# Experts' combination, final norm and the second mixer's norm in one stage over quarters of tokens

## The reference, cut to what matters

```python
# end of hier_moe: weighted sum of each token's two expert rows
y = yb[dest] * weights.reshape(-1)[order][:, None]
out = jax.ops.segment_sum(y, token_of, num_segments=t)
# end of the first block
x = x + g2x * hier_moe(...)
x = rmsnorm(x, final_norm_g)            # final norm of the first block
# start of the second block
h = x
z = rmsnorm_2(h, norm_mix_g[l]) @ w_in[l]     # the mixer's norm, then its input projection
...
h = h + jnp.concatenate([o_a, o_b, o_c], axis=-1) @ w_out[l]   # h is needed again here
```

## Time and profile before

| | |
|---|---|
| three runs | 4009.82, 4021.2, 4025.87 us; median 4021.2 |
| span of the profiled execution, first to last instruction | 4008.8 us |
| PE busy | 3340.9 us, 83% of the span |
| DVE busy | 2156.3 us, 54% |
| ACT busy | 1273.0 us, 32% |
| mean granted TensorE clock | 0.907 |
| bytes read and written | 449.40 MB and 79.38 MB |

### The profile page before, as it was taken

The page is one execution under the profiler, slowest core; times in us unless marked ns, Lnnn a source line. Parts: engine busy times, 40 slices in busy tenths (PEclk is TensorE's granted clock), DMA queues, the critical chain, the costliest instruction groups (busy, mean ns, idle before and its releaser), DMA issues. The chain is left out here.

```text
span 4008.8 us, 52023 instructions
## 1 busy us (share of the span) xinstructions
PE 3340.9 (83%) x18856; PEld 2686.1 (67%) x18856; DVE 2156.3 (54%) x3042; ACT 1273.0 (32%) x1914; POOL 210.2 (5%) x301
## 2 busy tenths in 40 slices
PE   5799884775969999996699868859488989998977
PEld 2688672664738888885488767638267877787755
DVE  3211643444359999997411175376436765776443
ACT  3201211335058888885300042421221110110011
POOL 1000000132001111110000000000000000000000
PEclk8899995788979999997899989969799999999988
DMA  6232641384149579995132212000203322332221
GB/s 241 72 93 65 180 150 57 96 224 142 44 172 374 204 261 382 373 359 186 43 104 89 74 66 61 27 29 4 79 16 94 94 80 86 96 93 80 68 63 42
DMA packets 381401, 507.45 MB, mean 127 GB/s; under 512 B 48218, under 2 KB 288465, under 8 KB 377953
## 3 DMA queue, kind: packets, MB, share of 16 engines
q1 hardware_dynamic: 342928, 439.80, 32.6%
q10 hardware_dynamic: 25856, 46.67, 3.3%
q0 software_dynamic: 12496, 19.35, 1.4%
HBM read 449.40 MB, written 79.38 MB: 132 GB/s over the span
## 5 line engine op out<-in xcount | busy, mean ns | idle before, releaser
L1923 DVE TENSOR_TENSOR exp_w_lo<-exp_w_raw,exp_w_hi 128x1024 fp32r<-128x1024 f32 x378 | 435.5, 1218 | 5.1
L1871 ACT ACTIVATE exp_w_hi<-exp_w_raw 128x1024 fp32r<-128x1024 f32 x378 | 371.0, 1055 | 7.7 <-PE exp_up_psum L339 7.7
L337 PE MATMUL in_ps_psum<-hN_hi,in_wh 128*128 128x512 f32 x704 | 276.4, 393 | 38.3 <-DVE in_wl L331 38.3
L337 PE MATMUL up_ps_psum<-hN_hi,up_wh 128*128 128x512 f32 x704 | 281.1, 399 | 31.0 <-DVE up_wl L331 31.0
L338 PE MATMUL up_ps_psum<-hN_lo,up_wh 128*128 128x512 f32 x704 | 280.7, 399 | 0.0
L339 PE MATMUL up_ps_psum<-hN_hi,up_wl 128*128 128x512 f32 x704 | 280.4, 398 | 0.0
L338 PE MATMUL in_ps_psum<-hN_lo,in_wh 128*128 128x512 f32 x704 | 275.8, 392 | 0.0
L339 PE MATMUL in_ps_psum<-hN_hi,in_wl 128*128 128x512 f32 x704 | 275.4, 391 | 0.0
L329 DVE CAST in_wh<-in_w 128x1024 fp32r<-128x1024 f32 x44 | 30.5, 694 | 424.2 <-PE in_ps_psum L339 414.2
L337 PE MATMUL exp_up_psum<-exp_w_hi,exp_x_hi 128*128 128x512 f32 x592 | 231.7, 391 | 3.6 <-DVE exp_w_lo L1923 3.6
L339 PE MATMUL exp_up_psum<-exp_w_hi,exp_x_lo 128*128 128x512 f32 x592 | 231.5, 391 | 0.0
(11 more groups left out here) (626 smaller groups left out, 7643.9 us busy)
## 6 DMA issues: line engine op xcount, KB each, us to landing
exp_w_raw<-in_expert_w_in SPq DMA_DIRECT2D x256, 512.0 KB, 5.7
up_w<-in_ffn_up SPq DMA_DIRECT2D x88, 512.0 KB
exp_w_raw<-in_expert_w_out SPq DMA_DIRECT2D x64, 512.0 KB, 7.0
hF<-in_expert_w_out SPq DMA_DIRECT2D x64, 512.0 KB, 7.3
ada_w<-in_ada_w SPq DMA_DIRECT2D x24, 1024.0 KB, 9.2
in_w<-in_w_in SPq DMA_DIRECT2D x44, 512.0 KB, 4.3
down_w<-in_ffn_down SPq DMA_DIRECT2D x44, 512.0 KB
wout_w<-in_w_out SPq DMA_DIRECT2D x16, 512.0 KB, 3.7
```

The costliest lines, as they stand in the source:

```text
L337: pe.matmul(out, r(w[0]), r(x[0]), start=start, stop=False)
L1871: act.activation(wh[:, c, :].bitcast(F32R), raw[c], ACT.Copy).then_inc(s_wh, 1)
L1923: dve.tensor_tensor(wl[:, c, :].bitcast(F32R), raw[c], wh[:, c, :], ALU.subtract).then_inc(s_wl[c], 1)
```

## The change

The three stages of combination, final norm and mixer's norm become one stage over four quarters of 256 tokens (two tiles each). The final norm is no longer written to `hF` there: the stage reads the un-normed `hF`, makes both means from one set of squares (a second matrix `gw` holds g1²/1024), writes the mixer's input (high and low) and keeps the first reciprocal root in `K.root1`. The normed `hF` is made later, by DVE, inside "in2" (`beside`, 16 instructions of 128x512). ACT's argument `aside` of `stage_gemm_f`, which nothing used, goes. The tiles of the routing plan stay allocated until the projection has ended.

```diff
@@ stage_gemm_f, list of DVE
                 weights(1, 0)
+                if beside is not None:
+                    beside(dve)
                 with dve.Fori(0, npair - 1) as i:
@@ stage_combine(K, x, gcol, g1, g2): list of ACT
+                def squares(q):
+                    act.wait_ge(s_h, 2 * q + 2)
+                    if q >= 2:
+                        act.wait_ge(s_st, q - 1)
+                    act.activation(sq[q % 2][:], cols(K.hF, q), ACT.Square).then_inc(s_sq, 1)
+
+                def first_root(q):
+                    u = q % 2
+                    act.wait_ge(s_st, q + 1)
+                    act.activation(ln1[u][:], p1[u][:, 0:QT], ACT.Ln, bias=K.c("eps")).then_inc(s_ln, 1)
+                    act.wait_ge(s_ln, q + 1)
+                    act.activation(inv1[u][:], ln1[u][:], ACT.Exp, scale=-1.0).then_inc(s_iv, 1)
+                    act.activation(K.root1[:, q * QT:(q + 1) * QT], ln1[u][:], ACT.Exp, scale=-0.5).then_inc(s_iv, 1)
+
+                def second_root(q):
+                    u = q % 2
+                    act.wait_ge(s_mx, q + 1)
+                    act.activation(ln2[u][:], ln2[u][:], ACT.Ln, bias=K.c("eps")).then_inc(s_l2, 1)
+                    act.wait_ge(s_l2, q + 1)
+                    act.activation(ln2[u][:], ln2[u][:], ACT.Exp, scale=-0.5).then_inc(s_rt, 1)
+
+                def high(q):
+                    act.wait_ge(s_x, 8 * q + 8)
+                    act.activation(cols(x[0], q).bitcast(F32R), tmp[q % 2][:], ACT.Copy).then_inc(s_hi, 1)
+                act.preload_act_table_set("natural_log_exp_and_others")
+                for i in range(3):
+                    weighted(i)
+                for q in range(NQ):
+                    squares(q)
+                    for i in (2 * q + 3, 2 * q + 4):
+                        if i < NT:
+                            weighted(i)
+                    first_root(q)
+                    second_root(q)
+                    if q:
+                        high(q - 1)
+                high(NQ - 1)
@@ list of DVE
+                def mixed(q):
+                    u = q % 2
+                    dve.wait_ge(s_iv, 2 * q + 2)
+                    dve.tensor_tensor(ln2[u][:], p2[u][:, 0:QT], inv1[u][:], ALU.mult).then_inc(s_mx, 1)
+
+                def normed(q):
+                    u = q % 2
+                    dve.wait_ge(s_rt, q + 1)
+                    dve.tensor_tensor(rr[u][:], ln2[u][:], K.root1[:, q * QT:(q + 1) * QT], ALU.mult).then_inc(s_mx2, 1)
+                    dve.wait_ge(s_mx2, q + 1)
...
+                    for k in range(KT):
+                        dve.scalar_tensor_tensor(tmp[u][:, k, :], cols(K.hF, q)[:, k, :], g12[:, k:k + 1], rr[u][:], ALU.mult, ALU.mult).then_inc(s_x, 1)
+
+                def low(q):
+                    dve.wait_ge(s_hi, q + 1)
+                    dve.tensor_tensor(cols(x[1], q).bitcast(F32R), tmp[q % 2][:], cols(x[0], q), ALU.subtract).then_inc(s_lo, 1)
+                dve.tensor_tensor(gsq[:], g1, g1, ALU.mult).then_inc(s_gn, 1)
+                dve.tensor_tensor(g12[:], g1, g2, ALU.mult).then_inc(s_gn, 1)
+                dve.wait_ge(s_gn, 2)
+                for k in range(KT):
+                    dve.tensor_scalar(gw[:, k, :], K.c("mean1024"), gsq[:, k:k + 1], None, ALU.mult).then_inc(s_gn, 1)
+                for i in range(2):
+                    summed(i)
+                for q in range(NQ):
+                    added(2 * q)
+                    if 2 * q + 2 < NT:
+                        summed(2 * q + 2)
+                    added(2 * q + 1)
+                    if 2 * q + 3 < NT:
+                        summed(2 * q + 3)
+                    if q:
+                        normed(q - 1)
+                    mixed(q)
+                    if q:
+                        low(q - 1)
+                normed(NQ - 1)
+                low(NQ - 1)
@@ list of PE
+                def means(q):
+                    u = q % 2
+                    pe.wait_ge(s_sq, q + 1)
...
+                    for k in range(KT):
+                        pe.matmul(p1[u][:, 0:QT], K.c("mean1024"), sq[u][:, k, :], start=k == 0, stop=k == KT - 1)
+                    for k in range(KT):
+                        mm = pe.matmul(p2[u][:, 0:QT], gw[:, k, :], sq[u][:, k, :], start=k == 0, stop=k == KT - 1)
+                    mm.then_inc(s_st, 1)
+                for i in range(3):
+                    turn(i)
+                for q in range(NQ):
+                    if 2 * q + 3 < NT:
+                        turn(2 * q + 3)
+                    means(q)
+                    if 2 * q + 4 < NT:
+                        turn(2 * q + 4)
@@ mixer_two(K, x)
-        x = tuple(K.sb(f"hN3_{x}", [P, KT, T], stack=norm) for x in ("hi", "lo"))
-        stage_norm(K, "nm", K.hF, x, T, K.cols[:, K.col_at["norm_mix_g_2"]:K.col_at["norm_mix_g_2"] + 8])
+        def residual_normed(dve):
+            for h in range(2):
+                t = slice(h * BANK, (h + 1) * BANK)
+                for k in range(KT):
+                    dve.scalar_tensor_tensor(K.hF[:, k, t], K.hF[:, k, t], K.col("final_norm_g", k), K.root1[:, t], ALU.mult, ALU.mult)
```

More of the change, by code:

```diff
@@ L451, in _, with stage_gemm_f @@
                     ada_vector(dve)
-def stage_gemm_f(K, name, groups, src, ntok, whole=None, residual=None, gcol=None, ctx=None, aside=None):
+def stage_gemm_f(K, name, groups, src, ntok, whole=None, residual=None, gcol=None, ctx=None, beside=None):
     npair = sum(g[1] for g in groups) // (2 * P)
@@ L533, in _ @@
                         mm.then_inc(s_mm[u], 1)
[L535 to L538, removed]
             if residual is None:
@@ L1948, in _, with stage_combine @@
                     rest_up(b, UP[3:])
-def stage_combine(K, gcol):
+def stage_combine(K, x, gcol, g1, g2):
     nc = K.nc
     yb = K.scratch["moe_y"]
-    NT, NB = T // P, 3
+    NT, NB, NQ = T // P, 3, 4
+    QT = T // NQ
     with K.stage() as st:
         U = range(2)
-        a = [[K.sb(f"comb_{k}_{u}", [P, D], stack=st) for u in range(NB)] for k in range(2)]
+        sb = lambda n, shape: K.sb(f"comb_{n}", shape, stack=st)
+        a = [[sb(f"{k}_{u}", [P, D]) for u in range(NB)] for k in range(2)]
+        sq, tmp = [sb(f"sq{u}", [P, KT, QT]) for u in U], [sb(f"tmp{u}", [P, KT, QT]) for u in U]
+        ln1, inv1, ln2, rr = ([sb(f"{n}{u}", [P, QT]) for u in U] for n in ("ln1", "inv1", "ln2", "root"))
+        gsq, g12, gw = sb("gain_sq", [P, KT]), sb("gains", [P, KT]), sb("gain_mean", [P, KT, P])
         pt = [K.ps(f"comb_ps{u}", [P, 2, 4, P], st) for u in U]
+        p1, p2 = ([K.ps(f"comb_{n}{u}", [P, BANK], st) for u in U] for n in ("mean", "gmean"))
         s_g = [[K.sem(f"comb_in{k}{u}") for u in range(NB)] for k in range(2)]
-        s_m, s_w, s_t, s_h = K.sem("comb_second"), K.sem("comb_sum"), K.sem("comb_turned"), K.sem("comb_added")
+        s_m, s_w, s_t, s_h, s_gn, s_sq, s_st, s_ln, s_iv, s_mx, s_l2, s_rt, s_x, s_hi, s_lo = (K.sem(f"comb_{n}") for n in (
+            "second", "sum", "turned", "added", "gains", "squares", "means", "log", "inverse", "mixed", "log2", "root", "normed", "hi", "lo"))
+        s_mx2 = K.sem("comb_roots")
+        cols = lambda t, q: t[:, :, q * QT:(q + 1) * QT]
         with nc.Block() as block:
@@ L1971, in _, with weighted @@
             def _(act):
-                for i in range(NT):
+                def weighted(i):
                     act.wait_ge(s_g[1][i % NB], 16 * (i // NB + 1))
                     act.activation(a[1][i % NB][:], a[1][i % NB][:], ACT.Copy, scale=K.moe_w[:, 1, i:i + 1]).then_inc(s_m, 1)
+                def squares(q):
[3 more added lines that the diff above has]
+                    act.activation(sq[q % 2][:], cols(K.hF, q), ACT.Square).then_inc(s_sq, 1)
@@ L1976, in _, with summed @@
+                high(NQ - 1)
             @block.vector
             def _(dve):
+                def summed(i):
+                    u = i % NB
+                    dve.wait_ge(s_g[0][u], 16 * (i // NB + 1))
+                    dve.wait_ge(s_m, i + 1)
+                    dve.scalar_tensor_tensor(a[0][u][:], a[0][u][:], K.moe_w[:, 0, i:i + 1], a[1][u][:], ALU.mult, ALU.add).then_inc(s_w, 1)
                 def added(i):
@@ L1993, in _, with turn @@
+                normed(NQ - 1)
+                low(NQ - 1)
             @block.tensor
             def _(pe):
-                for i in range(NT):
+                def turn(i):
                     u = i % 2
@@ L2008, in moe @@
     g = lambda n: K.cols[:, K.col_at[n]:K.col_at[n] + 8]
[L2009 to L2031, removed]
@@ L2032, in moe, with requests @@
-    stage_norm(K, "nf1", K.hF, K.hF, T, g("final_norm_g"))
+    plan = K.mixer_norm = K.stack.enter_context(ExitStack())
+    K.moe_w = K.sb("moe_w", [P, 2, T // P], stack=plan)
+    K.moe_xi, K.moe_yi = (K.sb(f"moe_{x}_rows", [P, NBLK + 2], I32, stack=plan) for x in "xy")
+    K.blk_at, K.blk_of = K.sb("blk_at", [P, NE + 1], I32, stack=plan), K.sb("blk_of", [P, NBLK + 2], I32, stack=plan)
```

(34 more changed lines are left out.)

6 lines of the change are left out of this document (added).

## The result

| | before | after |
|---|---|---|
| median of 20 runs | 4016.38 us (4009.49 to 4028.98) | 4028.24 us (4022.24 to 4042.83) |
| span of the profiled execution | 4008.8 us | 4029.9 us |
| first load of the combination to the end of the mixer's norm | 93.71 us | 114.56 us |
| first load to the first matmul of in2 | 100.73 us | 121.95 us |

The ratio is 1.0028, 95% interval [1.0019, 1.0038]: 8 to 15 us slower. The interval leaves out 1, so it is slower, and still within the 0.5% that the prediction called no difference. The profiled executions of the two are 21.1 us apart, the medians 11.9. Both need explaining.

The account below looks back on a forecast made before the run. DVE bounds the combination, waiting chains the norms. From 1877.5, quarters of 21.9, 54.0 (two) and 26.3 us end the stage at 1979.7 against 1957.2: +22.5 on the 4021.2 median gives 4043.7, say 4044; range 4025 to 4065.

Parts of the forecast that it names:

- The chain of a quarter: Merged stage: squares, turn, means, roots, mix, rounding and low part follow in list order, 27.0 us for quarters 1 and 2.
- Means: PE in each quarter: 32 matmul records, 0.427 us apart at 1.2 GHz, then 0.213 at 2.4 GHz; 8.3 us, last quarter 9.2.
- rival 2: PE's means in the merged stage: clock stays at 1.2 GHz throughout, 20.5 us more, end +43, 4064 us; chance 0.12.
- The Trainium skill's sentence on unsaturated engines: Merged stage: smaller instructions may finish sooner on unsaturated engines, so one square of 2048 before the means is the wrong size.
- Rival 1: Merged stage: DVE's work covers the chain if squares to roots take under 5.0 us; 23 us faster, 3998; chance 0.07.
- The cover of gains, table load and small instructions: Stage start and in2: ten small DVE gains, ACT's 1.3 us table load and 16 gains of 10.6 us cost nothing.
- The total: Whole program: 22.5 us later, 4043.7 us, say 4044; chances slower 0.57, same 0.36, faster 0.07.
- Rival 4: PE's means: clock rises at once or steps are shorter, means 6.8 us, +15.6, 4037, counted as no difference; chance 0.16.
- The base: Whole program: median taken as 12.4 us over the 4008.8 us span, 4021.2 us, and the stage difference added to it.

Follow-up runs that it names:

- the reordered one: Changed kernel with its ACT, DVE and PE lists reordered, no instruction more or less: median 3994.05 us, ratio 0.9947 to before; with last quarter's rounding halved too, 3986.67, 0.9923.
- no_gains: Changed kernel without the 16 DVE gains in in2: first matmul to end of in2's first block 12.92 us, against 13.13 to 13.20.
- the shifted one: Kernel before plus 17 DVE maxima of 128x1024 at the end of the combination: median 4042.77 us, ratio 1.0067.
- one_mean: Changed kernel with seven of eight matmuls of the second mean left out: first load to first matmul of in2 109.02 us.

## Why the prediction was right or wrong

**The chain of a quarter: right, 1.5 us too long in all.** Squares to low part in the order written, by its steps and as measured in quarter 1, from the second addition: means start 6.1 (6.0), mix starts 16.1 (15.5), the rounding 17.4 (16.9), the low part ends 21.6 (21.1). Last additions ended at 1877.59, 1899.67, 1926.08 and 1951.74 against a forecast of 1877.5, 1899.4, 1926.4 and 1953.4. The third period was 1.3 us too long in the sum: it counted a sum of a tile 8 that does not exist. The stage ended at 1978.24 against 1979.7. DVE stood 11.96, 7.54, 7.99 and 9.45 us for its mixes, where "some 8" was written, and 2.8 before the first three low parts, where 3 was (1.98 before the last).

**Means: right in size.** At a granted clock of 1.00 (2.4 GHz) it was 0.216 between loads, against 0.213. Each set of 32 took 7.9 to 9.4 us by its loads, where 8.3 and 9.2 stood in the sum. The granted clock rose within each set, so rival 2 (low throughout, 4064) did not come about: over the first mean's 16 loads, which took 4.41 to 5.92 us, it was 0.55 to 0.75, over the second's, 3.43 us in all four quarters, 1.00. The Trainium skill's sentence on unsaturated engines ("Perfetto Trace Analysis", "Optimizing Scalar/DVE Operations") is borne out in the tail, where two halves of rounding and low part beat the whole ones by 1.9 us. Ahead of the means it was not tried; there the order cost more than the size, since the square was 1.91 of the 6.0 us.

**Rival 1: its mechanism fits; its number agrees partly by luck.** It was to decide once the time from the last addition to the mix was covered by DVE's other work. The kernel as changed has 3.7 + 1.3 us of such work against 15.5; the reordered one has two additions, two sums, a low part and gains, and its stage is 24 us shorter than the old three (69.57 against 93.71), where the rival's arithmetic had 23. In that arithmetic the last additions end 44.2 us after the first load and 26.3 us of tail follow; in the reordered kernel they ended at 48.0 and 21.6 followed, so two errors nearly cancel. No run varied the cover around the 5.0 us at which the rival was to set in, so that threshold is not shown. What the prediction did not say is how cheap that case was to reach.

**The cover of gains, table load and small instructions: right.** For the gains see no_gains. At the start of the merged stage ACT still stood 2.17 us and DVE 2.75 us for the first data after their table load and small instructions.

**The total: wrong.** Forecast +22.5 us (0.56%), measured 0.28% [0.19, 0.38], later 0.38% and 0.34% with intervals of 0.22 to 0.50%: 8 to 20 us. The measured 4028.24 lies in the stated range of 4025 to 4065, near its lower end, but the likeliest outcome was given as slower (0.57) and it came out within the 0.5% of "same" (0.36). Rival 4 had put a case there, by means of 6.8 us; they took 7.9 to 9.4, so it is not that. The step that failed is the last of the sum, "The median of the runs is 12.4 us over that span, and I add the difference to the median": the 22.5 us between a calculated stage and the stage of one execution were taken as the difference of the medians, which was 11.9 us. Four things lie between, as far as the runs show:

1. The sum of the chain was 1.5 us too long, and the first profile of before had the shortest stretch of three: 100.73, then 102.91 and 102.63, against 121.95, 122.36 and 123.03. The mean difference is 122.4 - 102.1 = 20.4 us, not 22.5.
2. The last stage, which the change does not touch, is 2.1 us shorter in the three profiles of the changed kernel (see the last section). Together 18.3 us.
3. The rest of the program, from the first matmul of in2 on, took 2038.0 to 2055.3 us in four profiles of before and of the shifted one (mean 2045.6) and 2036.9 to 2049.6 in nine with the change in some form (mean 2042.0): 3.6 us less, those of the last stage among them. The spread within each is larger than the difference.
4. The profiled executions are not typical of all. Their spans, 4008.8, 4024.7 and 4002.5 for before and 4029.9, 4030.8 and 4028.5 for the changed kernel, have means 17.7 us apart. All executions timed in the comparisons above, 114 of before and 44 of the changed kernel, have means of 4016.1 and 4029.1, which are 13.0 apart. And the two kernels do not scatter alike: the middle half of before lies between 4010 and 4022 us, that of the changed kernel between 4027 and 4031. In before the time goes with the granted clock: the eight executions at a mean clock of 0.902 took 4020.8 to 4028.2 us, the eleven at 0.909 took 4004.3 to 4011.2.

So the traces say about 17 us, the medians of the three comparisons 11.9, 14.2 and 15.9, and their intervals reach from 8 to 20. The forecast of 22.5 lies outside; its mechanism was right and its size too large, by 6.6 to 10.6 us against the three medians. Why the kernel before scatters more was not settled. The windows attention alone can differ by 9 us between two executions of one kernel, but with one trace for each run it cannot be said how often it does so in either kernel.

**The base.** The three runs shown had a median of 4021.2 us, 20 runs 4016.38, with values from 4009 to 4029. A forecast in absolute time carried this too: with +22.5 on 4016.4 it would have been 4038.9 instead of 4043.7.

## What to carry to other kernels

When stages are merged, write out for each engine what stands in its list between the start of a dependent chain and its result, and compare it with the chain's length: here 5 us of cover against 15.5, four times over, ate a saving that the busy times promised, and the saving came back when only the order was changed. A merge takes out barriers and passes but also turns two concurrent flows of small pieces into one chain of large ones; put the next portion's independent work ahead of each wait, and cut the last portion small. And before one profiled execution is made the base of a forecast of a few tenths of a per cent, find out how far two executions of the same kernel lie apart, here 22 us in span.

## What the runs showed of the hardware that was not expected

The last stage (turning and storing the output) is the same code in all kernels. From DVE's first copy to its last it took 15.9 us in three profiles (two of before, one of the shifted kernel), 15.4 in the third of before, 15.2 in one_mean and 13.6 in the remaining eight. Two of the lines with DVE's copies in the timeline of before:

```profile
3996.11 2.45 DVE L3228 COPY out_rows<-out_ps_psum 128x1024 f32<-128x1024 f32 x2 [2.72 <-DMA out<-out_rows]
4000.09 2.50 DVE L3228 COPY out_rows<-out_ps_psum 128x1024 f32<-128x1024 f32 x2 [1.53 <-DMA out<-out_rows]
```

And two from the timeline of after:

```profile
4016.86 1.23 DVE L3338 COPY out_rows<-out_ps_psum 128x1024 f32<-128x1024 f32 x1 [0.47 <-DMA out<-out_rows]
4019.11 1.23 DVE L3338 COPY out_rows<-out_ps_psum 128x1024 f32<-128x1024 f32 x1 [1.03 <-DMA out<-out_rows]
```

In before the copies come in pairs, and each pair waits for a store; in after they wait one by one, for less. The DMA view of that stage has one packet on queue q8, marked as instructions, in the slower profiles and none on it in the faster ones. The line of before (packets, MB, share of the 16 engines):

```profile
q8 instruction: 1, 0.02, 0.5%
```

The two go together in all 13 profiles: each with the packet took 15.2 us or more, each without it 13.6. That a kernel's code length, by where such a load falls, sets the rhythm of its last stores is a reading; no run moved the packet alone.
